# One run of 512 columns for the joined matmuls of the second MLP product

## What is computed

```python
h = rms_norm(x, g_mlp) * (1.0 + scale2) + shift2
ff = jnp.square(jax.nn.relu(h @ w_ff1)) @ w_ff2      # w_ff1 1024x4096, w_ff2 4096x1024
return x + gate2 * ff
```

## Time and profile before

| | us |
|---|---|
| median of 3 runs | 1403.32 (1403.24 to 1403.36) |
| the profiled execution, its own time | 1403.55 |
| its span, first to last instruction | 1401.8 |
| second MLP product, first to last matmul | 925 to 1393 |
| steps 0 to 19, with the joined matmuls | 925.14 to 1256.08 |
| mean granted TensorE clock | 1.000 |

### The profile page before, as it was taken

How to read it: one execution, slowest core, us unless ns; L and a number is a source line. 1 busy time by engine, 2 the same in 40 slices (tenths; PEclk the granted TensorE clock), 3 DMA queues, 4 the chain that set the end, 5 groups by cost and what they waited for, 6 DMA issues and landing times.

```text
span 1401.8 us, 18026 instructions
## 1 busy us (share of the span) xinstructions
PE 1379.7 (98%) x7332; PEld 1170.7 (84%) x7332; DVE 812.8 (58%) x781; ACT 588.1 (42%) x703; POOL 478.0 (34%) x269
## 2 busy tenths in 40 slices
PE   5999999999999999999999999999999999999998
PEld 3877778898888888888888888888888888888887
DVE  5967688795438974555334453353746434354584
ACT  5667888665325632332222222342322223423152
POOL 0002111145003775574554545531432222333131
PEclk9999999999999999999999999999999999999999
DMA  9444411106210343343433334479997444445552
GB/s 368 170 158 158 155 63 38 46 31 215 116 61 31 120 162 124 137 146 140 152 122 114 127 141 152 166 276 388 377 388 285 151 150 155 167 173 197 200 189 90
DMA packets 75699, 231.27 MB, mean 165 GB/s; under 512 B 5729, under 2 KB 9953, under 8 KB 66786
## 3 DMA queue, kind: packets, MB, share of 16 engines
q1 hardware_dynamic: 75074, 229.60, 44.6%
q10 hardware_dynamic: 544, 0.52, 0.1%
HBM read 165.09 MB, written 65.01 MB: 164 GB/s over the span
## 4 chain that ended last, share of the span: by engine, by line
PE 95%; DVE 2%; DMA 1%; SPq 1%; issue 1%; ACT 0%; POOL 0%; DVEq 0%; ACTq 0%
PE bank L827 19%; PE bank L828 19%; PE bank L829 19%; PE bank L821 9%; PE bank L822 9%; PE bank L823 9%; PE bank L837 5%; PE bank L838 3%; DMA mod_first<-in_w_mod 1%; PE bank L866 1%; PE bank L878 0%; DVE two_r L2194 0%; SPq L590 0%; DVE n_t L2166 0%; PE bank L848 0%
## 5 line engine op out<-in xcount | busy, mean ns | idle before, releaser
L2585 POOL TENSOR_TENSOR w_lo<-w_raw,w_hi 128x2048 fp32r<-128x2048 f32 x28 | 134.7, 4812 | 319.6 <-ACT w_hi L1644 318.1
L2312 DVE TENSOR_TENSOR hin_two<-hin,hin_two 128x3072 fp32r<-128x3072 f32 x28 | 130.3, 4657 | 187.7 <-ACT hin_two L1656 187.7
L827 PE MATMUL bank<-hin_two,w_lo 128*128 128x512 f32 (+1 forms) x576 | 211.4, 367 | 0.0
L828 PE MATMUL bank<-hin_two,w_hi 128*128 128x512 f32 (+1 forms) x576 | 210.8, 366 | 0.0
L829 PE MATMUL bank<-hin_two,w_hi 128*128 128x512 f32 (+1 forms) x576 | 210.5, 365 | 0.0
L1644 ACT ACTIVATE w_hi<-w_raw 128x2048 fp32r<-128x2048 f32 x28 | 53.6, 1915 | 247.3 <-PE bank L838 150.2
L2577 POOL TENSOR_TENSOR w_lo<-w_raw,w_hi 128x512 fp32r<-128x512 f32 x43 | 65.4, 1520 | 183.8 <-ACT w_hi L1582 183.7
L827 PEld LDWEIGHTS bank<-hin_two,w_lo 128*128 128x128 f32 x576 | 108.6, 189 | 18.2 <-issue 0.2
L829 PEld LDWEIGHTS bank<-hin_two,w_hi 128*128 128x128 f32 x576 | 108.6, 189 | 17.7
L828 PEld LDWEIGHTS bank<-hin_two,w_hi 128*128 128x128 f32 x576 | 108.7, 189 | 17.0 <-issue 0.2
L1592 ACT ACTIVATE hid<-bank 128x768 f32<-128x768 f32 (+2 forms) x68 | 52.5, 773 | 162.8 <-PE bank L829 152.6
(11 more groups left out here) (297 smaller groups left out, 3473.5 us busy)
## 6 DMA issues: line engine op xcount, KB each, us to landing
hin<-hid_all SPq DMA_DIRECT2D x28, 1536.0 KB, 6.6
hid_all<-hid SPq DMA_DIRECT2D x105, 384.0 KB, 2.5
w_raw<-in_w_ff SPq DMA_DIRECT2D x36, 1024.0 KB, 9.1
mod_raw<-in_w_mod SPq DMA_DIRECT2D x16, 1024.0 KB, 6.0
w_raw<-in_w_ff SPq DMA_DIRECT2D x60, 256.0 KB, 3.2
x<-in_xT SPq DMA_DIRECT2D x5, 2048.0 KB, 14.3
w_sums<-w_raw SPq DMA_DIRECT2D x8, 1024.0 KB, 15.6
w_raw<-w_sums SPq DMA_DIRECT2D x8, 1024.0 KB, 9.7
```

The lines of the kernel that those rows point to most:

```text
L827: pe.matmul(out, w_lo, v_hi, start=first, stop=False, skip_group_check=True)
L828: pe.matmul(out, w_hi, v_lo, start=False, stop=False, skip_group_check=True)
L2312: dve.tensor_tensor(hin_part(n % 3, LO), hin[n % 3][:].rearrange("p t n -> p (t n)"), hin_part(n % 3, HI), ALU.subtract).then_inc(hin_lo_d ...
L2585: pool.tensor_tensor(w2_lo[n % 2][:].rearrange("p t n -> p (t n)"), w2_raw[m % RAWS][:].rearrange("p t n -> p (t n)"), w2_hi[n % 2][:].rea ...
```

## The change

The high and low parts are laid in one piece of 4 tiles x 1536 columns for each buffer. In a tile the columns are: 0 to 511 the low part of the 512, 512 to 767 the low part of the 256, 768 to 1023 the high part of the 256, 1024 to 1535 the high part of the 512. The load puts the raw values where the low parts go, so each tile's 768 columns (3,072 bytes) lie 6,144 bytes apart. The joined matmul reads columns 512 to 1023 as one run. The two splits become two instructions each, of 4 x 512 and 4 x 256 columns, and only the second signals. The first load waits for P6 in place of P5. Buffer 2 moves. A wait of ScalarE on the stores of the first product's results, ahead of the split for n = 2, goes. The other call sites only change how the two parts are passed, and the mixer's `three_of` becomes `three`, with the same matmuls.

```diff
-    hin_at = (A0 + 98304, A0 + 73728, A0 + 110592)
-    hin_apart = (36864, 12288, 12288)
-    hin = [place(f"hin{i}", [P, GF, HTOK], F32, o) for i, o in enumerate(hin_at)]
-    hin_two = [place(f"hin_two{i}", [P, 2, n // 4], F32R, o) for i, (o, n) in enumerate(zip(hin_at, hin_apart))]
...
+    hin_at = (A0 + 98304, A0 + 73728, A0 + 122880)
+    hin = [place(f"hin{i}", [P, GF, 2 * HTOK], F32, o) for i, o in enumerate(hin_at)]
+    hin_two = [place(f"hin_two{i}", [P, GF, 2 * HTOK], F32R, o) for i, o in enumerate(hin_at)]
+    WIDE, NARROW = (0, CH), (CH, QC)
+    def hin_raw(i, o, size):
+        return hin[i][:, :, o:o + size]
+    def hin_lo(i, o, size):
+        return hin_two[i][:, :, o:o + size]
+    def hin_hi(i, o, size):
+        at = HTOK if o else HTOK + QC
+        return hin_two[i][:, :, at:at + size]
+    def hin_both(i, t):
+        return hin_two[i][:, t, CH:CH + 2 * QC]
...
             if n < 3:
-                sp.wait_ge(ff1_mm, 7 * (NJ - 1) + (P5, P3, P6)[n] + 1)
+                sp.wait_ge(ff1_mm, 7 * (NJ - 1) + (P6, P3, P6)[n] + 1)
...
-            sp.dma_start(hin[n % 3][:], hid_d[j, :, GF * g:GF * (g + 1)]).then_inc(ld_hin[n % 3], 16)
+            sp.dma_start(hin_raw(n % 3, 0, HTOK), hid_d[j, :, GF * g:GF * (g + 1)]).then_inc(ld_hin[n % 3], 16)
...
-        def three_apart(out, w_hi, w_lo, v, first, last):
-            pe.matmul(out.rearrange("p (h n) -> p h n", h=2), w_hi, v, start=first, stop=False, skip_group_check=True)
-            return pe.matmul(out[:, HI * QC:(HI + 1) * QC], w_lo, v[:, HI], start=False, stop=last,
+        def three_apart(out, w_hi, w_lo, v_both, first, last):
+            pe.matmul(out, w_hi, v_both, start=first, stop=False, skip_group_check=True)
+            return pe.matmul(out[:, QC:2 * QC], w_lo, v_both[:, QC:2 * QC], start=False, stop=last,
                              skip_group_check=True)
...
-            elif n == 2:
-                for j in range(7):
-                    act.wait_ge(st_hid[j], 16 * NJ)
-            else:
+            elif n > 2:
                 act.wait_ge(ff2_mm, products_before(n - 2))
-            act.activation(hin_part(n % 3, HI), hin[n % 3][:].rearrange("p t n -> p (t n)"), ACT.Copy).then_inc(hin_hi_done, 1)
+            for part in (WIDE, NARROW):
+                m = act.activation(hin_hi(n % 3, *part), hin_raw(n % 3, *part), ACT.Copy)
+            m.then_inc(hin_hi_done, 1)
...
-            dve.tensor_tensor(hin_part(n % 3, LO), hin[n % 3][:].rearrange("p t n -> p (t n)"),
-                              hin_part(n % 3, HI), ALU.subtract).then_inc(hin_lo_done, 1)
+            for part in (WIDE, NARROW):
+                m = dve.tensor_tensor(hin_lo(n % 3, *part), hin_raw(n % 3, *part), hin_hi(n % 3, *part), ALU.subtract)
+            m.then_inc(hin_lo_done, 1)
```

More of the change, by code:

```diff
@@ L829, in three_more @@
             return pe.matmul(out, w_hi, v_hi, start=False, stop=last, skip_group_check=True)
-        def three_of(out, w_hi, w_lo, v, first, last):
-            return three_more(out, w_hi, w_lo, v[:, HI], v[:, LO], first, last)
-        def three_apart(out, w_hi, w_lo, v, first, last):
-            pe.matmul(out.rearrange("p (h n) -> p h n", h=2), w_hi, v, start=first, stop=False, skip_group_check=True)
-            return pe.matmul(out[:, HI * QC:(HI + 1) * QC], w_lo, v[:, HI], start=False, stop=last,
+        def three_apart(out, w_hi, w_lo, v_both, first, last):
+            pe.matmul(out, w_hi, v_both, start=first, stop=False, skip_group_check=True)
+            return pe.matmul(out[:, QC:2 * QC], w_lo, v_both[:, QC:2 * QC], start=False, stop=last,
                              skip_group_check=True)
@@ L1007, in pq @@
                         o = (n + 2 * s * t) * P
-                        m = three_of(bank[PQ_BANKS[f][i]][:, o:o + P], fold_hi[f][:, t, cols],
-                                     fold_lo[f][:, t, cols], ab[:, :, t, f, :], True, True)
+                        m = three(bank[PQ_BANKS[f][i]][:, o:o + P], fold_hi[f][:, t, cols], fold_lo[f][:, t, cols],
+                                  ab[:, HI, t, f, :], ab[:, LO, t, f, :], True, True)
                 m.then_inc(pq_mm, 1)
@@ L1135, in ff1_product @@
                     w = slice(kk * P, (kk + 1) * P)
-                    m = three_of(out, w1_hi[o % 4][:, w], w1_lo[o % 4][:, w], pair[:, :, kk],
-                                 i in (P1, P5, P2, P3) and kk == 0, kk == FT - 1)
+                    m = three_more(out, w1_hi[o % 4][:, w], w1_lo[o % 4][:, w], pair[:, HI, kk], pair[:, LO, kk],
+                                   i in (P1, P5, P2, P3) and kk == 0, kk == FT - 1)
             m.then_inc(ff1_mm, 1)
@@ L1181, in ff2_step @@
                         last = (g == GF - 1 or n == NSTEP - 3 and (k, i) == (1, 1)) and t == GF - 1
-                        v = hin_pair(n % 3, t, o, size)
                         if j < NSPLIT and size == QC:
-                            m = three_apart(bank[k][:], w2_hi[n % 2][:, t, w], w2_lo[n % 2][:, t, w], v, first, last)
-                        else:
-                            m = three_of(ps[:, at:at + size], w2_hi[n % 2][:, t, w], w2_lo[n % 2][:, t, w], v,
-                                         first, last)
+                            m = three_apart(bank[k][:], w2_hi[n % 2][:, t, w], w2_lo[n % 2][:, t, w],
+                                            hin_both(n % 3, t), first, last)
+                        else:
+                            m = three_more(ps[:, at:at + size], w2_hi[n % 2][:, t, w], w2_lo[n % 2][:, t, w],
+                                           hin_hi(n % 3, o, size)[:, t], hin_lo(n % 3, o, size)[:, t], first, last)
                     at += size
@@ L1196, in last_part @@
                     w = slice(dd * P, (dd + 1) * P)
-                    m = three_of(ps[:, at:at + size], w2_hi[n % 2][:, t, w], w2_lo[n % 2][:, t, w],
-                                 hin_pair(n % 3, t, o, size), late and n == NSTEP - 2 and t == 0,
-                                 only and t == GF - 1)
+                    m = three_more(ps[:, at:at + size], w2_hi[n % 2][:, t, w], w2_lo[n % 2][:, t, w],
+                                   hin_hi(n % 3, o, size)[:, t], hin_lo(n % 3, o, size)[:, t],
+                                   late and n == NSTEP - 2 and t == 0, only and t == GF - 1)
                 at += size
```

## The result

| us | before | changed |
|---|---|---|
| median of 22 runs each | 1403.47 | 1405.61 |
| range, one run of 6371.32 before left out | 1403.24 to 1405.30 | 1404.68 to 1407.22 |
| the profiled execution | 1403.55 | 1404.80 |
| its span | 1401.8 | 1403.0 |

The ratio is 1.0014, 95% interval 1.0007 to 1.0020: the change made the kernel slower, and its median is outside the range of the prediction (1399.8 to 1404.6).

The account below looks back on a forecast made before the run. TensorE, busy for 98% of the span, was taken to bound the kernel. 1403.55 + 0 for the pairs + 0.1 for the feed gave 1403.65 us for the profiled execution, 1403.4 against the median; range 1399.8 to 1404.6.

Parts of the forecast that it names:

- The excess of 0.0125 us a pair: Second MLP product: a long-short matmul pair costs 0.3525 us against 0.340 at best; 320 pairs bound the gain at 4.0 us.
- the ideal first pair: First pair of a step, after one-run matmuls: 0.34 us despite its two runs, so the runs are not the cause.
- the tail behind a chain of 256-column matmuls: Five one-run matmuls after such a chain take 1.16 us in place of 1.133, 0.027 too much without two-run matmuls near.
- half: Rival on the pairs: part of the excess is due to the two runs; 1.5 us less, 1401.8 us; chance 14%.
- all: Rival on the pairs: the whole excess is due to the two runs; 3.2 us less, 1400.1 us; chance 15%.
- the pair that pays in full: Slower rival: one-run pairs each pay the whole 0.027 us; 4.6 us more over 320 pairs, 1408.0 us; chance 7%.
- I take 0.3: Load in four pieces of 3,072 bytes per partition: 0 to 0.43 us more for a load, taken as 0.3.
- The thin places at the fourth and fifth step: Feed of TensorE with cover of 0.85 and 1.13 us, asked for 0.96 and 1.1; +0.1 us taken, 0.5 at the dear end.
- one more costs 0.16 us: VectorE's split: a second instruction adds 0.16 us fixed cost; with ScalarE's 0.20, low part 0.36 us later, hidden in steady steps.
- the work of these engines in it under 5 us: ScalarE and VectorE in a 16.5 us step of the second MLP product: work under 5 us, so added split time is hidden.
- The mishap that had 2%, a feed that fails: Case in which the feed of TensorE fails by over 2.8 us at the places with thin cover; chance 2%.
- a wait of TensorE over 1 us anywhere in the steps: Sign in the changed kernel's profile, steps of the second MLP product, that would prove the prediction wrong on the feed.

Follow-up runs that it names:

- the first experiment: The kernel before with only VectorE's split of the hidden values in two instructions (2048 and 1024 columns), old layout: 1404.5 us, ratio 1.0005 against the kernel before.

## Why the prediction was wrong

**Right: what a pair costs.** The excess of 0.0125 us a pair has nothing to do with the two runs. It stayed at 5.64 us for 16 pairs with one run, and went down to 5.54 us with two runs and another order. The reading of the earlier trace rows, the ideal first pair and the tail behind a chain of 256-column matmuls, held. The three rivals on TensorE (half, all, and the pair that pays in full) are out.

**Right: the load, the moved wait, the dropped wait.** The term "I take 0.3" fits a single load, 6.9 us to landing for 6.6, but it does not add up over loads: after three of the new kind the splits that wait for them begin 0.3 to 0.4 us later, not 0.9, and in the run with nothing but these and the one-run matmuls no time is lost. The thin places at the fourth and fifth step (n = 3 and n = 4) were named rightly and cost together 0 to 0.14 us in the five traces of the new layout, for 0.1. ScalarE's copy of P7 begins at 918.03, for the 918.2 that were worked out, and TensorE does not wait for it.

**Wrong: the splits.** The step that failed is "VectorE: ... one more costs 0.16 us. With the passing on, a step's low part is ready 0.36 us later." The fixed cost itself is about right: the two show 2.29 and 1.22 us, 0.15 us more than the 3.36 of one, and as they overlap a little they take 3.43 us together, 0.07 more. ScalarE's two take 2.86 us for 2.77. But the second one is not next in line any more. For n = 4 to 7 ScalarE hands GpSimd its work while VectorE's first instruction runs, and the second then waits out a whole weight split: 5.6 us in place of 1.22, a term of 4.4 us and not of 0.16. The profile before had the signs. GpSimd's 5.99 us for a weight split, against 4.63 in a window without such an overlap, is a wait behind VectorE's 3.36 us instruction. And VectorE's 28 splits have a mean of 4657 ns on the page, not 3360: from n = 9 to n = 25 GpSimd starts first, and VectorE stands until it is done (5.22 to 5.24 us). Both raise the question who goes first if VectorE's instruction is cut in two.

In the Trainium skill (SBUF — State Buffer, Who interferes with whom) this is a rule: an instruction of VectorE with two inputs in SBUF and one of GpSimd that reads SBUF share a port under an exclusive lock, and "Issue order, not op shape, decides who blocks." By the page's section "SBUF: two separate sides" whichever starts first has the lock for its whole instruction. The traces agree as to the blocking (5.6 against 1.22 us for VectorE's second instruction, 5.63 to 5.99 against 4.6 us for GpSimd's). As to the order there is one exception: in the first experiment, for n = 5, GpSimd's instruction began at 1002.29, before VectorE's second, and still had to wait for it.

**Wrong with it: how far to look for thin cover.** The prediction took "the work of these engines in it under 5 us" for all steps, from the one window of n = 2. The windows of n = 3 and n = 4 in the kernel before show more, since sums of weights and the twelve result adds stand there on VectorE too (its busy time is the fourth column):

```profile
974.78:991.33 16.55, 16.55 (x82) 13.91 (x81) 13.24 (x13) 4.64 (x3) 5.99 (x1) 1.00 1.03 406
991.33:1007.88 16.55, 16.55 (x83) 13.91 (x81) 11.62 (x7) 4.64 (x2) 5.63 (x1) 1.00 0.97 361
```

The prediction asked for a wait where the cover is thin now (0.85 and 1.13 us at n = 3 and n = 4) and did not look at n = 5, with 3.1 us of cover for the weights and 7.5 us for the values. The loss came there, because two delays of 4.4 us stood one behind the other on VectorE, and the adds and sums between them gave only 0.5 us back. The prediction's own sign, "a wait of TensorE over 1 us anywhere in the steps", is there: step n = 5 starts 1.37 us late. The mishap that had 2%, a feed that fails, was sized at over 2.8 us, and a loss of 1.4 us was in none of the cases. Against the sum: 1403.4 was forecast, with +0.1 for the feed. The median is 1405.1, and the two traces have 1.5 and 1.6 us of the 1.7 us in the steps n = 3 to 5.

**Open.** Why a 256-column matmul costs its neighbours up to 0.027 us was not settled, only that the access pattern is not the reason. What decides which of the two engines goes first at n = 5 is not known: GpSimd comes 2.17 us after VectorE in the run in which it lost and in the ones in which it won. In runs without a trace the order was not seen, so it is not shown either that it makes the spread of 1.4 us in the first experiment, or of 1 us in the changed kernel.

## What to carry to other kernels

An instruction cut in two is not the same work plus a fixed cost: each gap is a place where another engine can get its turn, as GpSimd did here, and the second half then waits for all of the other's instruction. Look for instructions that show longer than they take alone, as GpSimd's 5.99 for 4.6 us and VectorE's 5.22 for 3.36 us did, and ask who goes first after the edit; hold the other engine back by a wait if the order matters. Check the cover in each step, not in one that is taken for all. And before a layout is changed to make a matmul's operand one run, compare starts rather than durations: here the order of long and short matmuls was worth 2 us, the layout nothing.

## What the runs showed that was not expected

- A matmul whose 512 columns come in two runs of 256, far apart, costs the same as one with a single run: 0.2269 against 0.2267 us between starts.
- Short matmuls are cheapest in a row. 16 long and 16 short ones take 5.64 us in turn and 5.54 us sorted; spread singly among long ones, a short one costs 0.004 us more than in turn.
- GpSimd's instruction that comes 2.17 us after the start of a VectorE instruction of 2.28 us, 0.1 us before its end, mostly goes ahead of VectorE's next one (7.85 or 7.86 us for VectorE's two in seven cases, n = 5 and n = 6 in four traces), and once did not (3.42 us).
- The 1.5 us of the longer runs are TensorE's clock. In three of the ten traces the granted clock is at its lower level (1.2 GHz) for part of the window from 26 to 31 us (mean 0.66), and the 16 matmuls there that read `mod_first` take 3.40 to 3.43 us; in the others it is 1.00 and they take 1.92 or 1.93 us. In the experiments' runs of the kernel before, which fall into two groups with a gap from 1403.80 to 1404.63 us, the mean clock is 0.997 or 0.998 in every longer run and 0.999 or 1.000 in every other; the other kernels' runs are divided by it. TensorE had waited for a load just before, 1.27 to 1.29 us in the three and 0.80 to 1.29 us in others, so the wait alone does not tell which it will be.
